# Hybrid diffusion backbone: low parts of the experts' weights on VectorE alone, and a ring of sixteen slots

## What is computed

```python
gate, idx = lax.top_k(aff.T, cap)
xe = xt[idx]
hg = jnp.einsum("ecd,edf->ecf", xe, w_g)
hu = jnp.einsum("ecd,edf->ecf", xe, w_u)
y = jnp.einsum("ecf,efd->ecd", jax.nn.silu(hg) * hu, w_d)
y = y * gate[..., None].astype(y.dtype)
out = jnp.zeros_like(xt).at[idx.reshape(-1)].add(y.reshape(-1, D))
```

## Time and profile before

| | before |
|---|---|
| median of 3 runs | 3039.09 us |
| the profiled execution | 3039.95 us |
| its span | 3038.1 us |
| mean granted clock | 0.960 |
| PE busy | 2699.2 us (89%) |
| DVE busy | 1934.6 us (64%) |
| ACT busy | 1579.7 us (52%) |
| POOL busy | 869.8 us (29%) |
| moved by DMA | 595.91 MB, mean 196 GB/s |

### The profile page before, as it was taken

One profiled execution on the slowest core, in us unless ns is written; L12 is line 12 of the kernel. 1 busy time (PEld: TensorE's weight loads), 2 busy tenths in 40 slices (PEclk: granted clock), 3 DMA queues, 4 the chain that ended last, 5 costly groups with the idle time before them and its releaser, 6 DMA issues.

```text
span 3038.1 us, 40777 instructions
## 1 busy us (share of the span) xinstructions
PE 2699.2 (89%) x13616; PEld 1916.1 (63%) x13616; DVE 1934.6 (64%) x2879; ACT 1579.7 (52%) x2282; POOL 869.8 (29%) x529
## 2 busy tenths in 40 slices
PE   6879999999995899999987999999999499999994
PEld 1248777777774565655657777777777356666562
DVE  6864356545337788888875346653435688888884
ACT  5543344333322677777763444433422377777774
POOL 0003000212121455555541200031122155555553
PEclk8879999999998999999998999999999799999997
DMA  9842011111232899999993211121233399999996
GB/s 334 322 141 87 28 39 56 49 51 54 99 104 108 291 365 356 364 357 359 359 340 109 72 32 35 35 77 35 63 117 127 132 351 365 366 361 364 361 357 222
DMA packets 191609, 595.91 MB, mean 196 GB/s; under 512 B 23008, under 2 KB 33054, under 8 KB 191478
## 3 DMA queue, kind: packets, MB, share of 16 engines
q1 hardware_dynamic: 172726, 529.76, 48.1%
q0 software_dynamic: 18640, 64.20, 7.1%
q10 hardware_dynamic: 112, 0.23, 0.0%
HBM read 568.88 MB, written 25.23 MB: 196 GB/s over the span
## 4 chain that ended last, share of the span: by engine, by line
PE 54%; issue 17%; DVE 9%; POOL 8%; DMA 6%; ACT 5%; POOLq 0%; SPq 0%; ACTq 0%; DVEq 0%
PE bank L447 14%; PE bank L449 13%; PE bank L448 12%; POOL low L1891 6%; PE bank L816 4%; PE bank L788 4%; DMA ring<-in_w_e_up 3%; ACT high L1002 2%; PE bank L806 2%; DVE low L1304 2%; POOL x_resid L1906 1%; DMA ring<-in_w_mod 1%; POOL U L1884 1%; PE bank L619 1%; PE bank L620 1%
## 5 line engine op out<-in xcount | busy, mean ns | idle before, releaser
L1002 ACT ACTIVATE high<-ring 128x1024 fp32r<-128x1024 f32 (+1 forms) x1012 | 1058.9, 1052 | 520.4 <-PE bank L449 279.5
L1708 DVE TENSOR_TENSOR low<-ring,high 128x1024 fp32r<-128x1024 f32 (+1 forms) x564 | 838.6, 1522 | 191.0 <-ACT high L1002 189.8
L1891 POOL TENSOR_TENSOR low<-ring,high 128x1024 fp32r<-128x1024 f32 (+1 forms) x194 | 509.0, 2624 | 595.7 <-ACT high L1002 580.3
L447 PE MATMUL bank<-high,hT_high 128*128 128x512 f32 (+2 forms) x1280 | 519.7, 406 | 25.7 <-ACT sigr L1088 13.6
L449 PE MATMUL bank<-high,hT_low 128*128 128x512 f32 (+2 forms) x1280 | 485.4, 379 | 0.0
L448 PE MATMUL bank<-low,hT_high 128*128 128x512 f32 (+2 forms) x1280 | 484.0, 378 | 0.0
L447 PE MATMUL bank<-high,xeT_high 128*80 128x512 f32 x1024 | 411.6, 402 | 32.0 <-POOL low L1891 29.7
L448 PE MATMUL bank<-low,xeT_high 128*80 128x512 f32 x1024 | 402.8, 393 | 0.0
L449 PE MATMUL bank<-high,xeT_low 128*80 128x512 f32 x1024 | 401.9, 392 | 0.0
L1304 DVE TENSOR_TENSOR low<-ring,high 128x1024 fp32r<-128x1024 f32 (+2 forms) x254 | 303.5, 1222 | 139.2 <-ACT high L1002 137.8
L1189 ACT ACTIVATE att<-bank,st 128x640 f32<-128x640 f32 (+3 forms) x200 | 136.5, 683 | 351.4 <-DVE st L1563 256.8
(11 more groups left out here) (238 smaller groups left out, 3324.5 us busy)
## 6 DMA issues: line engine op xcount, KB each, us to landing
ring<-in_w_e_down SPq DMA_DIRECT2D x260, 512.0 KB, 5.2
ring<-in_w_e_gate SPq DMA_DIRECT2D x256, 512.0 KB, 6.0
ring<-in_w_e_up SPq DMA_DIRECT2D x256, 512.0 KB, 6.9
ring<-in_w_mod SPq DMA_DIRECT2D x96, 512.0 KB, 6.3
ring<-in_w_gate SPq DMA_DIRECT2D x64, 512.0 KB, 3.8
ring<-in_w_in SPq DMA_DIRECT2D x24, 512.0 KB, 5.0
ring<-in_w_branch SPq DMA_DIRECT2D x16, 512.0 KB, 4.3
ring<-in_w_out SPq DMA_DIRECT2D x16, 512.0 KB, 5.0
```

What stands on the lines that cost most here:

```text
L447: nc.tensor.matmul(out, lhs[0], rhs_high, start=start, stop=False)
L1002: A(high[:, g % HIGH, :, 0:w], ring[:, g % RING, :, 0:w], ACT.Copy).then_inc(high_done, 1)
L1708: V.tensor_tensor(low[:, (g + HIGH) % RING, :, 0:w], ring[:, (g + HIGH) % RING, :, 0:w], high[:, g % HIGH, :, 0:w].bitcast(F32), ALU.subtr ...
L1891: G.tensor_tensor(low[:, g % RING, :, 0:w], ring[:, g % RING, :, 0:w], high[:, g % HIGH, :, 0:w].bitcast(F32), ALU.subtract).then_inc(low_ ...
```

## The change

VectorE makes the low parts of all chunks, and GpSimd keeps only the gathers and scatters. In the expert stages the ring has 16 slots (`RING_E`) and `high` has eight (`HIGH_E`); in the other stages both stay at 8 and 4. Slots 8 to 15 of the ring lie in `att`, which now follows the ring directly: 8 to 12 in words 0 to 5119, free when attention is over, and 13 to 15 in words 5120 to 8191, free when `xn` has been transposed and stored. The four new slots of `high` lie in `hT`, free after the router. `plan_ring` works out for each chunk its slot, how often this slot was filled, and which chunk must be used before. `SLOT_E` starts with slots 8 to 12, so five expert chunks can be loaded while `w_out`'s eight chunks still hold slots 0 to 7.

SP now has gate of expert 0 and up of expert 0 ahead of its loop and waits for `o_ev` (all attention units evacuated) before the first of them, and for `norm_tr` and `xn_out` before slot 13. ACT and DVE make four more parts before the first rows (`range(HIGH, HIGH_E)`), ACT once `lg_full` tells that the router's logits are done. In the last expert of a layer the next layer's four chunks are split at j = 8 to 11 instead of 12 to 15, and the four unused loads at the end are gone. `rows_high` moves from j = 3 to 2, `rows_low` from 4 to 3. POOL's `expert` begins with the gather.

The core of the diff:

```diff
-def by_pool(g):
-    l, c = divmod(g - CH_MOD, CH_LAYER)
-    return g >= CH_MOD and g % 4 == 3 and (c >= CH_DENSE or (c < HIGH and l > 0))
+RING_E = 16
+HIGH_E = 8
+SLOT_E = [8, 9, 10, 11, 12, 0, 1, 2, 3, 4, 5, 6, 7, 13, 14, 15]
+def plan_ring():
+    slot, fills, free, hslot, hfree = [], [], [], [], []
+    count, last, hlast = [0] * RING_E, [None] * RING_E, [None] * HIGH_E
+    for g in range(N_CHUNKS):
+        e = (g - CH_MOD) % CH_LAYER - CH_DENSE if g >= CH_MOD else -1
+        a, h = (SLOT_E[e % RING_E], e % HIGH_E) if e >= 0 else (g % RING, g % HIGH)
+        count[a] += 1
+        slot.append(a)
+        fills.append(count[a])
+        free.append(None if last[a] is None else last[a] + 1)
+        hslot.append(h)
+        hfree.append(None if hlast[h] is None else hlast[h] + 1)
+        last[a] = hlast[h] = g
+    return slot, fills, free, hslot, hfree
...
# SP, matrix()
-                        sp.wait_ge(ring_used, i * (2 * CH_EXP) + (g + k - RING + 1))
+                        if i is not None:
+                            sp.wait_ge(ring_used, i * (2 * CH_EXP) + SLOT_FREE[g + k])
+                        elif SLOT_FREE[g + k] is not None:
+                            sp.wait_ge(ring_used, SLOT_FREE[g + k])
+                        if i is None and g == g0 and k == 0:
+                            sp.wait_ge(o_ev, N_UNIT * (l + 1))
+                        if i is None and SLOT[g + k] == 13:
+                            sp.wait_ge(norm_tr, 2 * T * (2 * l + 2))
+                            for b in range(2):
+                                sp.wait_ge(xn_out[b], xn_store(l, 4 - b))
...
-            for j in range(HIGH):
-                g = N_CHUNKS + j
-                fill(g % RING, w_chunk(w_e_down[L - 1, NE - 1], 0, NW, j), g - RING + 1)
...
# PE, split_done()
-                s, n = (low_pool, LOW_POOL[g]) if by_pool(g) else (low_dve, LOW_DVE[g])
+                pe.wait_ge(low_dve, g + 1 if i is None else i * (2 * CH_EXP) + (g + 1))
...
# ACT, expert() and ahead of it
-                        split_high(g + HIGH, i, NEXT_W if last and l + 1 < L and j >= 4 * NQ - HIGH else NW)
+                        if not last or j < CH_GATE0:
+                            split_high(g + HIGH_E, i)
+                        elif l + 1 < L and j < CH_GATE0 + HIGH:
+                            split_high(chunk_no(l + 1, j - CH_GATE0))
+                act.wait_ge(lg_full, l + 1)
+                for j in range(HIGH, HIGH_E):
+                    split_high(g0 + j)
...
# DVE, expert() and ahead of it
-                        if not by_pool(g + HIGH):
-                            dve.wait_ge(high_done, i * (2 * CH_EXP) + (g + HIGH + 1))
+                        ahead = g + HIGH_E
+                        if last and j >= CH_GATE0:
+                            if l + 1 < L and j < CH_GATE0 + HIGH:
+                                split_low(chunk_no(l + 1, j - CH_GATE0))
+                        else:
+                            dve.wait_ge(high_done, i * (2 * CH_EXP) + (ahead + 1))
+                for j in range(HIGH, HIGH_E):
+                    split_low(g0 + j)
                 rows_low(0, 2 * NE * l)
...
# POOL, expert()
-                    for j in range(2 * HIGH + HIGH, (4 if last else 6) * NQ + 1, HIGH):
-                        split_low(g0 + at + j, i, NEXT_W if last and l + 1 < L and j == 4 * NQ else NW)
-                        if j == 4 * HIGH and rows:
-                            gather(e, i * 2 + (NE * l + e + 3))
+                    if rows:
+                        gather(e, i * 2 + (NE * l + e + 3))
                     pool.wait_ge(y_ready, n_exp + 2)
```

More of the change, by code:

```diff
@@ L261, in hybrid_step @@
         ring_at = nc.sbuf_base
[L262 to L265, removed]
+        sb("ring_mem", [P, RING * KC * NW])
         att_at = nc.sbuf_base
         att = sb("att", [P, 9952])
+        ring = nc.alloc_sbuf_tensor_at("ring", [P, RING_E, KC, NW], F32, offset=(ring_at + 31) // 32 * 32)
+        low = over("low", [P, RING_E, KC, NW], ring_at, 0)
+        high_at = nc.sbuf_base
+        sb("high_mem", [P, HIGH * KC * NW])
+        high = over("high", [P, HIGH_E, KC, NW], high_at, 0)
+        hT = [sb("hT_high", [P, KD, T * P], F32R), sb("hT_low", [P, KD, T * P], F32R)]
         U_at = nc.sbuf_base
@@ L491, in _, with fill @@
             sp.dma_start(mask_sw[:, :, :], k_mask_sw).then_inc(const_in, 16)
[L493 to L497, removed]
+            def fill(g, src, width=NW):
+                if SLOT_FREE[g] is not None:
+                    sp.wait_ge(ring_used, SLOT_FREE[g])
+                sp.dma_start(ring[:, SLOT[g], :, 0:width], src).then_inc(ring_full[SLOT[g]], 16)
             for g in range(CH_MOD):
@@ L542, in dense @@
                         g = chunk_no(l, n)
[L543 removed]
+                        fill(g, w_chunk(w, n0, width, kq), width)
                         n += 1
@@ L942, in matrix @@
                         for half in range(2):
-                            ins = three(bank(first + half)[0:CAP, :], stat(k), high[:, (g + k) % HIGH, half, :],
-                                        low[:, (g + k) % RING, half, :], k == 0, k == KD - 1)
+                            ins = three(bank(first + half)[0:CAP, :], stat(k), high[:, HSLOT[g + k], half, :],
+                                        low[:, SLOT[g + k], half, :], k == 0, k == KD - 1)
                         ins.then_inc(ring_used, 1)
@@ L1259, in expert @@
                         g = g0 + CH_GATE0 + e * CH_EXP + j
-                        if j == 3 and not last:
+                        if j == 2 and not last:
                             rows_high(1 - e, n_exp * 2 + 2)
@@ L1684, in expert @@
                         g = g0 + CH_GATE0 + e * CH_EXP + j
-                        if j == 4 and not last:
+                        if j == 3 and not last:
                             rows_low(1 - e, n_exp * 2 + 2)
@@ L1907, in expert @@
                                             in_=ybuf[0:CAP, e, :], in_offset=None, compute_op=ALU.add).then_inc(y_out, 16)
-                    if not last:
-                        for j in range(HIGH, 2 * HIGH + 1, HIGH):
-                            split_low(g0 + at + CH_EXP + j, i)
                     pool.wait_ge(y_out, n_exp * 16 + 16)
                     pool.sem_inc(added, 1)
-                split_low(g0)
                 gather(0, NE * l + 1)
@@ L1918, in _ @@
                 pool.wait_ge(gate2_in, 32 * (l + 1))
-                for j in range(HIGH, CH_GATE0 + 2 * HIGH + 1, HIGH):
-                    split_low(g0 + j)
                 with pool.Fori(0, LOOPED) as i:
@@ L1924, in _ @@
                 expert(0, LOOPED, rows=False)
-                expert(1, LOOPED, last=True, rows=False)
+                expert(1, LOOPED, rows=False)
             pool.dma_start(gfin_b, g_final.rearrange("(a n) -> a n", a=1).broadcast_to([P, D])).then_inc(gfin_in, 16)
```

73 lines of the change are left out of this document (30 added, 43 removed).

## The result

The changed kernel takes 2995.54 us (median of 4 runs, 2989.55 to 2999.54) against 3040.27 us (4 runs, 3035.56 to 3041.82): ratio 0.986, 95% interval 0.9843 to 0.9878. The forecast was 2973, its range 2952 to 3014. So the sign and the mechanism held and the size fell short, inside the range: 44.7 us came, 67 were forecast. The profiled executions are 3039.95 and 2989.55, 50.4 apart; this pair is used for the parts, and the one of after is the fastest of its four.

A forecast was written before the change was run, and what follows sets the result against it. PE was taken as the bound in the expert stages, losing 2.7 us per expert to waits. Savings of 32.6 us per stage plus 0.85 at the scatter, 67 over both layers, took 3039.95 to 2973 us, range 2952 to 3014.

The forecast's parts named there:

- What bounds the kernel: Expert stages: PE needs 34.0 us per expert but gets 36.7, losing 2.7 to waits for low parts and hidT.
- Low parts on DVE: Expert loop: without POOL's blocking each low part takes DVE 1.14 us, 32.1 per expert, fitting within PE's 34.0.
- hidT: Expert loop: PE still waits 0.7 us per expert for hidT's low part, bounds 0 and 0.75; period 34.8.
- Loads: Expert stages: DMA needs 35.0 us per expert, slightly over PE's 34.8, covered by a lead of 16 chunks.
- Extra loads before the stage at cost 0: Before the expert stage: weight loads issued early cost nothing, bounds 0 and 6 us.
- Four more splits at cost 0: Between top-k and experts: ACT's and DVE's four added splits fit idle time, DVE's being 6.27 us; bounds 0 and 1.
- The last expert: End of each expert stage: it takes 24.0 us against 29.3 measured before, with 4.3 for hid's round trip.
- Scatter 0.2 us after y: End of each stage: the last scatter follows y by 0.2 us instead of 1.05, 0.85 less.
- rival C: Expert loop: DVE reaches hidT, y or xeT late, 2 us per expert instead of 0.7; 3013 us, chance 0.12.
- A: Expert stages: DMA's mean rate is the ceiling, period stays 36.7, only the lead helps; 3010 us, chance 0.15.
- B: Expert stages: DVE's low parts stay at 1.54 us, 41.7 per expert, slower above 1.33; 3180 us, chance 0.05.
- D: Expert stages: the ring does not run ahead, loads bind at 35.5 us per expert; 3001 us, chance 0.05.

The follow-up runs named there:

- e7: e3 with hidT's high and low parts made one chunk earlier (j = 12 and 13); 2959.0 us, ratio 0.9746.
- e6: The changed kernel with POOL again making every fourth low part of the expert chunks, ring of 16 and eight high slots kept; 2997.7 us, ratio 0.9869.
- e5: The kernel before with VectorE making all low parts, ring still 8 slots and high parts 4; 3051.7 us, ratio 1.0060.
- e12: e5 with hidT's high and low parts made one chunk earlier; 3010.6 us, ratio 0.9913.
- e2: The changed kernel with 288 words of padding ahead of the high parts, which then begin at a multiple of 512 words; 2984.6 us, ratio 0.9817.
- e8: The changed kernel with the third of the three products left out in the experts; 2937.9 us, single run.
- e10: The changed kernel with four slots for high parts in place of eight, ring of 16 kept; 2990.7 us, ratio 0.9853.
- e1: The changed kernel with VectorE's four extra low parts moved behind the low parts of the first rows; 2986.7 us, ratio 0.9831.
- e4: The kernel before with 224 words of padding ahead of the high parts, so they lie at 224 modulo 512; 3047.1 us, ratio 1.0034.
- e3: The changed kernel with both the 288 words of padding and the four extra low parts behind the first rows; 2976.3 us, ratio 0.9801.
- e9: e7 with VectorE's product SiLU x up put ahead of chunk 7's low part in each layer's last expert; 2958.0 us, ratio 0.9737.

## Why the forecast was right in kind and 22 us off

The prediction counts experts from 1 where this part counts from 0: its experts 1 and 15 are 0 and 14 here.

- *What bounds the kernel.* PE's 34.0 us per expert: right, and shown by e7. The 2.7 us lost were low parts and hidT. But of the two reasons that I gave for late low parts, POOL's slowness and the late loads, the second is the one that counts in this order of work: the deeper ring with its eight high slots gives 1.5 of the 1.8 us although POOL keeps its low parts (e6), and taking these from POOL alone gives nothing (e5), since hidT then stands behind late chunks (e12). The wait bore POOL's name, but with the high parts earlier POOL, as slow as before, is in time. I never priced the two halves apart.
- *Low parts on DVE.* 1.14 us unblocked, mean 1220 ns: right. The sum of 32.1 us per expert: 465.31 us in 500, or 32.5 per 34.91.
- *hidT.* Forecast 0.7 per expert; e7 shows 0.6 (34.75 to 34.15). The period of 34.8 came out as 34.91, of which 0.16 is the address (e2). Term: 2 x 14 x 0.11 = 3 us.
- *Loads.* 35.0 per expert was too high by 1.4 (e8): by my guess since a gather costs less than the two steps that I read off beside one, which is not tested. Nothing hung on it, since the lead was to cover it.
- *Extra loads before the stage at cost 0.* No sign of a cost in the two profiles; the slower pace of `w_out`, 0.77 us per 119 matmuls, goes with the padding (e2). That a moved buffer could change the pace of an instruction was no term of the sum at all.
- *Four more splits at cost 0, bounds 0 and 1 per layer.* This failed. The idle 6.27 us of DVE were free, but not for POOL: the gather ran in them, and it takes no more than 0.96 us only if VectorE is still. It cost 3.5 and 3.8 us. I had used the port rule one paragraph earlier, for POOL's subtractions, and did not ask which other work of POOL it holds for.
- *The first part of the stage.* 51.2 us against 50.9 in layer 1: right.
- *The last expert.* 24.0 forecast, 26.4 measured, 4.8 us in two layers. The round trip of hid is 4.8 and not 4.3 (from the last up matmul, 1542.52, to the first down matmul, 1547.57, less one step), the pace adds 0.2, and behind the pause PE's matmuls are 0.43 us apart for 8 of them (granted clock 0.50 from 1549 to 1551), which costs 1.6. The pause of 3.06 us is itself longer than in the kernel before (2.35) and in e6 (2.29), where POOL has its low parts, and the same as in e10, where VectorE makes all of them with four high slots: so it comes with VectorE's extra work. Timelines of after, ACT, DVE and PE:
```profile
1543.01 1.06 ACT L1023 ACTIVATE high<-ring 128x1024 fp32r<-128x1024 f32 x1 [0.33 <-PE bank L468]
...
1544.10 1.23 DVE L1736 TENSOR_TENSOR low<-ring,high 128x1024 fp32r<-128x1024 f32 x1 [0.16 <-ACT high L1023]
1545.24 1.27 DVE L1716 TENSOR_TENSOR U<-sigr,bank 80x512 f32<-80x512 f32 x2
...
1547.83 0.60 PE L467 MATMUL bank<-low,hidT_high 128*80 128x512 f32 x1
1548.23 0.63 PE L468 MATMUL bank<-high,hidT_low 128*80 128x512 f32 x1
1548.66 0.63 PE L466 MATMUL bank<-high,hidT_high 128*80 128x512 f32 x1
```
  I counted this slow clock at the start of the stage and forgot it here, where the trace of before has it as well.
- *Scatter 0.2 us after y.* Wrong: y ends at 1561.94, the scatter begins at 1562.88, 0.94 later, with nothing between them. That is the hand-over itself; POOL's last low part in the earlier trace rows ended at the moment at which the scatter would have begun anyway. The term of 0.85 us in each layer is 0.1 or less.

The sum: forecast 67; less 5.0 and 4.4 in the two stages, 3.5 and 3.8 at the gathers, 0.85 at each of the two scatters, and about 1.5 per layer for the pace of `w_out` leaves 45.6. The medians give 44.7, with an interval of 37 to 48. The profiled pair gives 50.4, since it is 4.6 us ahead already at 188 us, in the modulation stage, which the change doesn't touch.

Two figures of the prediction were worked out wrong, and neither decides anything: rival C's 2973 and 39 are 3012, not 3013, and the low end of the forecast's own range, PE at 34.0, is 0.8 us less in each of 28 periods, so 2951 and not 2955.

Of the rivals, A falls (378, 387 and 394 GB/s where it had a ceiling of 358), B falls (1220 ns against the 1.33 us from which it decides, with ACT and DMAs at full work), D falls (no wait for a landing). C did not happen in the changed kernel but does with the short ring (e5).

## What to carry to other kernels

When a wait names a slow producer, ask when its input came: a deeper ring took away the wait for POOL's low parts while POOL stayed as slow as before, and taking the work from the slow producer alone made the kernel slower. On an engine that works in order, put what others wait for ahead of what waits for a transfer: hidT one place earlier was worth 17 us with the deep ring and 41 with the short one, for nothing. An idle engine is not a free one if it shares something with the engine that works in this gap, and a buffer that moves takes its alignment with it: when buffers are rearranged, compare the distance of two matmuls before and after in a stage that the change doesn't touch.

## What the runs showed of the hardware

- Fp32 subtractions of VectorE with two SBUF inputs (1.14 us each) hold POOL's issue of an indirect DMA: 0.96 us becomes 3.38 beside three in a row (e6) and 4.41 beside four, in both cases until 0.84 us after the last one's end; moved away, it is 0.97 (e1).
- fp32 matmuls with 512 columns at clock 1.00 start every 226.9 ns with `high` and `hT` at a multiple of 256 words from the ring's start, and every 231.0 (e4) to 233.4 ns (the changed kernel) at 224 modulo 512; in the experts 229.4 against 230.9.
- One core sustained 387 GB/s over 440 us of 512 KB loads with PE fully busy, and 394 when the loads were the limit.
- Behind a pause of 3.06 us in the last expert of layer 1, PE's matmuls are 0.43 us apart at a granted clock of 0.50, the 1.2 GHz level, for 6 (e3), 8 (the changed kernel) or 11 of them (e7); behind one of 1.71 us (e9) for 8 as well.
